# Plain norms transposed by products with a diagonal, their weight applied to feature columns: two transformer blocks on one Trainium2 core

## What is computed

```python
def _rms_norm(x, g):
    xf = x.astype(jnp.float32)
    y = xf * lax.rsqrt(jnp.mean(xf * xf, axis=-1, keepdims=True) + EPS)
    return (y * g.astype(jnp.float32)).astype(x.dtype)

for layer in range(DEPTH):
    hf = _swiglu(_rms_norm(x, g[0]), ...)
    x = x + 0.5 * _rms_norm(hf, g[1])
    xn = _rms_norm(x, g[2])
    mix = _attn_mixer(xn, ...) if layer % 2 == 0 else _mlstm_mixer(xn, ...)
    x = x + _rms_norm(mix, g[3])
    hf = _swiglu(_rms_norm(x, g[4]), ...)
    x = x + 0.5 * _rms_norm(hf, g[5])
```

## Time and profile before

| | us |
|---|---|
| median of 3 runs | 2288.61 |
| lowest, highest | 2287.96, 2290.32 |
| the profiled execution, its time | 2296.82 |
| the profiled execution, its span | 2294.6 |
| TensorE busy | 2102.6 |
| VectorE busy | 1347.0 |
| ScalarE busy | 1133.9 |

### The profile page before, as it was taken

One profiled execution on the slowest core, in us unless ns is written; L12 is line 12 of the kernel. 1 busy time (PEld: TensorE's weight loads), 2 busy tenths in 40 slices (PEclk: granted clock), 3 DMA queues, 4 the chain that ended last, 5 costly groups with the idle time before them and its releaser, 6 DMA issues.

```text
span 2294.6 us, 31170 instructions
## 1 busy us (share of the span) xinstructions
PE 2102.6 (92%) x13138; PEld 1825.3 (80%) x13138; DVE 1347.0 (59%) x1274; ACT 1133.9 (49%) x1455; POOL 446.4 (19%) x305
## 2 busy tenths in 40 slices
PE   7998977999899899699989977999998986999997
PEld 5898967999899898699978666777776875877775
DVE  5676336556665574655653656666666247565665
ACT  4765455565566354456543434454453244454553
POOL 2783000475166100036610000000000000000000
PEclk9999988999999898799999988999998787999999
DMA  9897514787688554278754105778886203688874
GB/s 325 290 310 236 168 56 135 243 280 251 210 287 277 154 167 138 94 240 293 264 175 151 56 10 211 280 287 321 340 295 222 83 1 146 235 313 316 321 290 177
DMA packets 224571, 495.98 MB, mean 216 GB/s; under 512 B 11816, under 2 KB 167576, under 8 KB 199696
## 3 DMA queue, kind: packets, MB, share of 16 engines
q1 hardware_dynamic: 200608, 410.20, 52.1%
q0 software_dynamic: 23552, 82.75, 10.6%
q10 hardware_dynamic: 272, 1.05, 0.1%
HBM read 486.57 MB, written 12.10 MB: 217 GB/s over the span
## 4 chain that ended last, share of the span: by engine, by line
PE 82%; DVE 9%; ACT 3%; DMA 3%; issue 2%; POOL 1%; DVEq 0%; SPq 0%; ACTq 0%
PE psum L972 79%; DVE nrm L2009 2%; DMA big<-in_ada_w 1%; DVE low L2009 1%; PE psum L1034 1%; DMA ring<-in_ffn_w_up 1%; PE psum L1555 1%; ACT wh L1644 1%; PE psum L1211 1%; DVE nrm L2075 0%; DVE xl L2009 0%; DVE nrm L2083 0%; DMA ring<-in_moe_w_gate 0%; DVE nrm L2073 0%; POOL big L744 0%
## 5 line engine op out<-in xcount | busy, mean ns | idle before, releaser
L2009 DVE TENSOR_TENSOR low<-ring,wh 128x2048 fp32r<-128x2048 f32 (+2 forms) x338 | 805.9, 2400 | 541.3 <-ACT wh L1644 540.2
L1644 ACT ACTIVATE wh<-ring 128x2048 fp32r<-128x2048 f32 (+2 forms) x338 | 640.6, 1903 | 430.2 <-PE psum L972 227.0
L972 PE MATMUL psum<-xh,wh 128*128 128x256 f32 x1832 | 521.6, 285 | 10.7 <-DVE low L2009 7.2
L972 PE MATMUL psum<-xl,wh 128*128 128x256 f32 x1832 | 520.8, 284 | 0.0
L972 PE MATMUL psum<-xh,low 128*128 128x256 f32 x1832 | 518.1, 283 | 0.0
L972 PEld LDWEIGHTS psum<-xh,wh 128*128 128x128 f32 x1832 | 352.8, 193 | 16.8 <-issue 9.9
L744 POOL TENSOR_TENSOR big<-big 128x1024 f32<-128x1024 f32 x144 | 306.0, 2125 | 240.9 <-ACT big L1721 232.9
L972 PEld LDWEIGHTS psum<-xl,wh 128*128 128x128 f32 x1832 | 350.9, 192 | 1.4
L972 PEld LDWEIGHTS psum<-xh,low 128*128 128x128 f32 x1832 | 351.1, 192 | 0.0
L972 PE MATMUL psum<-wh,xh 128*128 128x256 f32 (+5 forms) x864 | 278.5, 322 | 8.0 <-DVEq L647 6.0
L972 PE MATMUL psum<-wh,xl 128*128 128x256 f32 (+5 forms) x864 | 277.9, 322 | 0.0
(11 more groups left out here) (339 smaller groups left out, 2387.7 us busy)
## 6 DMA issues: line engine op xcount, KB each, us to landing
ring<-in_moe_w_gate SPq DMA_DIRECT2D x64, 1024.0 KB, 6.0
ring<-in_moe_w_up SPq DMA_DIRECT2D x64, 1024.0 KB, 6.3
ring<-in_moe_w_down SPq DMA_DIRECT2D x64, 1024.0 KB, 5.9
big<-in_ada_w POOLq DMA_DIRECT2D x48, 1024.0 KB, 6.7
ring<-in_ffn_w_gate SPq DMA_DIRECT2D x44, 1024.0 KB, 5.9
ring<-in_ffn_w_up SPq DMA_DIRECT2D x44, 1024.0 KB, 6.1
ring<-in_ffn_w_down SPq DMA_DIRECT2D x44, 1024.0 KB, 5.2
ring<-in_mlstm_w_in SPq DMA_DIRECT2D x16, 1024.0 KB, 5.5
```

The source lines that it names most:

```text
L972: return pe.matmul(out_, lhsT, rhs, start=start, stop=stop, **kw)
L1644: act.activation(wh[n % PARTS][:, 0:w], ring[SLOT_OF[n]][:, 0:w], ACT.Copy).then_inc(high, 1)
L2009: return dve.tensor_tensor(out_, a, b, op)
```

## The change

For the six plain norms (`by_columns`), `nrm` is no longer written. DVE makes, per tile, a 128x128 diagonal with the reciprocal roots on it. In the turn TensorE multiplies `x` itself by that diagonal (a real fp32 product in place of a transpose), so PSUM holds the transposed tokens already divided by their root. The norm's weight is loaded as one number per feature, [128, 8], and applied when the bank is emptied: ACT and DVE each make four instructions of 128x128 per quarter, with the weight of that feature group as a scale per partition, where each made one of 128x512. `gain_used` of the norm is raised after the turn instead of before it. The diff also carries a branch for norms with a shift (`column_vector`, `shifted`, `shifted_part`, three pieces of code); `by_columns` is false for all of them, so it does not run and is left out here.

```diff
+        def by_columns(s):
+            return STAGES[s][0] == "norm" and STAGES[s + 2][0] != "router" and not STAGES[s][1][0]
+        def diagonal(s, t):
+            g = sum(u for _, _, u in STAGES[:s])
+            return gain[g % GAINBUFS][:, P * (t + 1):P * (t + 2)]
@@ POOL, load_gain
-                pool.dma_start(gain[k % GAINBUFS][:, :], src).then_inc(gain_in[k % GAINBUFS], 16)
+                if k in COLUMNS:
+                    pool.dma_start(gain[k % GAINBUFS][:, 0:KT], GAINS[k].rearrange("(k p) -> p k", p=P),
+                                   allow_slow_non_contiguous=True)\
+                        .then_inc(gain_in[k % GAINBUFS], 16)
+                else:
+                    pool.dma_start(gain[k % GAINBUFS][:, :], src).then_inc(gain_in[k % GAINBUFS], 16)
@@ TensorE, turn
-                        last = pe.transpose(psum[:, q, i * P:(i + 1) * P], nrm[:, t, f:f + P], ident)
+                        if s and by_columns(s - 1):
+                            last = mm(psum[:, q, i * P:(i + 1) * P], x[:, t, f:f + P],
+                                      diagonal(s - 1, t), True, True)
+                        else:
+                            last = pe.transpose(psum[:, q, i * P:(i + 1) * P], nrm[:, t, f:f + P], ident)
@@ ACT, turn_columns
+                for q in range(4):
+                    tokens = slice((q // 2) * P, (q // 2 + 1) * P)
+                        act.wait_ge(turned, 4 * k + q + 1)
+                        for i in range(4):
+                            f = 4 * (q % 2) + i
+                            ins = act.activation(xh[:, f, tokens], psum[:, q, i * P:(i + 1) * P], ACT.Copy,
+                                                 scale=cols_[:, f:f + 1])
+                    ins.then_inc(turn_high, 1)
@@ DVE, norm_columns
+                for t in range(TT):
+                    dve.wait_ge(squared, SQ0[s] + t + 1)
+                    link(dve.reciprocal(stat[:, t:t + 1], stat[:, t:t + 1]))
+                    mark(dve.tensor_scalar(diagonal(s, t), ident, stat[:, t:t + 1], None, ALU.mult),
+                         normed, 2 * ran(s, "norm", "final") + t + 1)
@@ DVE, turn_columns
+                    for q in range(4):
+                        tokens = slice((q // 2) * P, (q // 2 + 1) * P)
+                        dve.wait_ge(turn_high, 4 * k + q + 1)
+                        for i in range(4):
+                            f = 4 * (q % 2) + i
+                            ins = dve.scalar_tensor_tensor(out=xl[:, f, tokens], in0=psum[:, q, i * P:(i + 1) * P],
+                                                           scalar=cols_[:, f:f + 1],
+                                                           in1=xh[:, f, tokens].bitcast(F32),
+                                                           op0=ALU.mult, op1=ALU.subtract)
+                        ins.then_inc(turn_low, 1)
+                dve.wait_ge(turn_low, 4 * k + 4)
+                for _ in range(STAGES[s - 1][2]):
+                    dve.nop().then_inc(gain_used, 1)
```

More of the change, by code:

```diff
@@ L623, in build, with shifted_part, shifts_before @@
         assert len(GAINS) == sum(s[2] for s in STAGES)
+        def by_columns(s):
[3 more added lines that the diff above has]
+            return gain[g % GAINBUFS][:, P * (t + 1):P * (t + 2)]
+        def shifted_part(q):
+            return nrm[:, q // 2, 512 * (q % 2):512 * (q % 2) + 512].rearrange("p (a b) -> p a b", a=4)
+        def shifts_before(s):
+            return sum(by_columns(j - 1) and STAGES[j - 1][1][0] is not None for j in range(1, s))
+        COLUMNS = {sum(u for _, _, u in STAGES[:s]) for s in range(len(STAGES)) if by_columns(s)}
         ada_w = [big[:, SLOT * i:SLOT * (i + 1)].rearrange("p (k n) -> p k n", k=KT) for i in range(2)]
@@ L1297, in spread_vector, with column_vector @@
                 return last
+            def column_vector(g, at):
+                wait_gain(pe, g)
+                for f in range(KT):
+                    last = mm(psum[:, 4, at + f:at + f + 1], gain[g % GAINBUFS][:, f * P:(f + 1) * P],
+                              const[:, C_ONES:C_ONES + 1], True, True)
+                return last
             def norm(s, k, m):
@@ L1302, in norm @@
                         pe.wait_ge(gate_copied, k_gate(s))
[L1303 to L1304 removed]
+                    if by_columns(s):
+                        column_vector(GAIN0[s] + 1, 0)
+                        column_vector(GAIN0[s] + 2, KT).then_inc(spread_pe, 1)
+                    else:
+                        spread_vector(GAIN0[s] + 1, 4)
+                        spread_vector(GAIN0[s] + 2, 6).then_inc(spread_pe, 1)
                 elif k == 1:
@@ L1669, in norm, with turn_columns @@
                     root_mean(stat[:, t:t + 1], D).then_inc(squared, 1)
+            def turn_columns(s, k):
+                g = GAIN0[s - 1]
+                cols_ = gain[g % GAINBUFS]
+                wait_gain(act, g)
+                for q in range(4):
+                    tokens = slice((q // 2) * P, (q // 2 + 1) * P)
+                    if STAGES[s - 1][1][0] is None:
+                        act.wait_ge(turned, 4 * k + q + 1)
[3 more added lines that the diff above has]
+                                                 scale=cols_[:, f:f + 1])
+                    else:
+                        act.wait_ge(shifted, 4 * shifts_before(s) + q + 1)
+                        ins = act.activation(xh[:, 4 * (q % 2):4 * (q % 2) + 4, tokens], shifted_part(q), ACT.Copy)
+                    ins.then_inc(turn_high, 1)
             def turn(s, k):
+                if by_columns(s - 1):
+                    return turn_columns(s, k)
                 for q in range(4):
@@ L2058, in place_pads, with norm_columns @@
                     dve.tensor_scalar(m, m, -1.0, None, ALU.mult)
+            def norm_columns(s, k, m):
+                g = GAIN0[s]
+                cols_ = gain[g % GAINBUFS]
+                wait_gain(dve, g)
+                if m is not None:
+                    dve.wait_ge(spread_pe, SPREAD0[s] + 1)
+                    dve.scalar_tensor_tensor(out=cols_[:, KT:2 * KT], in0=psum[:, 4, 0:KT], scalar=1.0,
+                                             in1=cols_[:, 0:KT], op0=ALU.add, op1=ALU.mult)
+                    link(dve.tensor_copy(cols_[:, 2 * KT:3 * KT], psum[:, 4, KT:2 * KT]))
+                for t in range(TT):
[3 more added lines that the diff above has]
+                         normed, 2 * ran(s, "norm", "final") + t + 1)
+                if k == 1:
+                    place_pads()
@@ new lines, in turn_columns, with low_of @@
+            def turn_columns(s, k):
+                g = GAIN0[s - 1]
+                cols_ = gain[g % GAINBUFS]
+                if STAGES[s - 1][1][0] is None:
+                    for q in range(4):
[8 more added lines that the diff above has]
+                        ins.then_inc(turn_low, 1)
+                else:
+                    def low_of(q):
+                        f, tokens = 4 * (q % 2), slice((q // 2) * P, (q // 2 + 1) * P)
+                        dve.wait_ge(turn_high, 4 * k + q + 1)
+                        tt(xl[:, f:f + 4, tokens], shifted_part(q), xh[:, f:f + 4, tokens].bitcast(F32),
+                           ALU.subtract).then_inc(turn_low, 1)
+                    for q in range(4):
+                        dve.wait_ge(turned, 4 * k + q + 1)
+                        for i in range(4):
+                            f = 4 * (q % 2) + i
+                            ins = dve.tensor_scalar(shifted_part(q)[:, i], psum[:, q, i * P:(i + 1) * P],
+                                                    cols_[:, KT + f:KT + f + 1],
+                                                    cols_[:, 2 * KT + f:2 * KT + f + 1], ALU.mult, ALU.add)
+                        ins.then_inc(shifted, 1)
+                        if q:
+                            low_of(q - 1)
+                    low_of(3)
+                dve.wait_ge(turn_low, 4 * k + 4)
+                for _ in range(STAGES[s - 1][2]):
+                    dve.nop().then_inc(gain_used, 1)
```

5 lines of the change are left out of this document (added).

## The result

| | before | after |
|---|---|---|
| median, us (same chip) | 2291.51 | 2302.2 |
| lowest, highest | 2287.96, 2298.0 | 2299.8, 2306.61 |
| ratio, 95% interval | 1 | 1.0044 (1.0028 to 1.006) |
| profiled execution, its span | 2294.6 | 2302.7 |
| TensorE busy, us | 2102.6 | 2113.6 |

The change makes the kernel slower by 0.44%, about 10 us (6 to 14). A second measurement of the same changed kernel gave 1.0052 (1.0039 to 1.0065). The forecast of 2288.4 meant no change, and its range of 2281 to 2296 doesn't hold the measured 2302.2.

A forecast was written before the change was run, and what follows sets the result against it. TensorE, busy 2102.6 of 2294.6 us, was taken as the bound, with pauses and half clock at seams. Start +1.3, five seams +7.5 and clock -9.0 gave -0.2 us: 2288.4 from the median of 2288.6, range 2281 to 2296.

The forecast's parts named there:

- Part 1: Each seam: TensorE starts the turn 1.67 us earlier, a reciprocal and a 0.24 us diagonal replacing VectorE's passes.
- Part 2: Turn at each seam: fp32 products take twice the transposes' time; third quarter ready after 24 passes, 5.38 us, 0.46 later.
- Part 3: Copies in four pieces at each seam: ACT's quarter 1.17 us (+0.56), VectorE's 1.12 (+0.42).
- Part 4: Clock at the seams: unbroken turn work brings full clock back before the weight products; -9.0 us together (-6 to -11).
- Part 5: Program start: the first turn ends later, delaying the first weight pieces and what follows; +1.3 us (0 to 3.4).
- (a): Rival, seams: the clock never falls, passes take 0.11 us; all five seams -10.5 us, 2278; chance 0.14.
- (b): Rival, seams: the clock doesn't come back during the turn, so its gain is gone; 2297.4 us; chance 0.10.
- (c): Rival, start: the first norm weight, loaded in 4-byte pieces, lands 6.8 us late; 2295 us; chance 0.06.
- (d): Rival, seams: copy pieces don't overlap, 4 us more, 2292.4, or 2295 with a poor mLSTM seam; chance beyond 2293 0.04.
- "Slower": Outcome for the whole kernel: measurably slower, where measurement tells apart about 0.2%, 4.6 us; chance 0.20.

The follow-up runs named there:

- e7: Kernel before, with fp32 products of `nrm` with the identity instead of transposes at the five seams; ratio 1.0006 (0.9992 to 1.002).
- e3: Kernel before, with four idle 128x512 VectorE additions ahead of the first turn's last subtraction; ratio 1.001 (0.9996 to 1.0024).
- e2: Changed kernel with only the first norm changed, the five seam norms as before; ratio 1.0019 (1.0003 to 1.0035).
- e4: Kernel before, with VectorE's two norm passes fused into one at the five seams and the last norm; ratio 0.998 (0.9968 to 0.9991).
- e9: Kernel before, with two idle 128x512 VectorE additions ahead of the first turn's last subtraction; ratio 1.0022 (1.0007 to 1.0038).
- e10: Kernel before, with four idle VectorE additions in the first turn and bias-row spreads held until the first gate piece is used; ratio 1.0014 (1.0003 to 1.0024).
- e11: Kernel before, with VectorE's two norm passes fused and bias-row spreads held until the first gate piece is used; ratio 0.9981 (0.9968 to 0.9994).
- e8: Kernel before, with ACT's and VectorE's copies in four pieces, scaled by ones, at the five seams; ratio 1.0038 (1.0021 to 1.0055).
- e1: Changed kernel with the first norm left as before, the five seam norms changed; ratio 1.0018 (1.0004 to 1.0032).
- e5: Changed kernel, with bias-row spreads held until the first gate piece is used; ratio 1.0044 (1.0029 to 1.006).
- e12: Changed kernel as it is, measured a second time against the kernel before; ratio 1.0052 (1.0039 to 1.0065).
- e13: Changed kernel, with bias-row spreads held until the first gate piece is used, measured a second time; ratio 1.0039 (1.0026 to 1.0052).

## Why the prediction was wrong

**Part 1 was right.** The turn starts 1.60 us earlier (3.34 to 1.74), forecast 1.67. The diagonal took 0.30 against 0.24.

**Part 2 was right.** 24 passes took 5.30 us, forecast 5.38. By itself the product costs 1.2 to 1.5 us in four seams and 2.3 in the first (e7).

**Part 3 was right.** ACT's quarter took 1.15 (1.17 forecast), VectorE's 1.14 (1.12). The sum of parts 1 to 3 was +7.5, and the five pauses grew by 6.3.

**Part 4 was the term that failed most: it was counted as -9.0 us, and the clock gave back nothing on balance.** That the new turn brings the clock up was right: behind all seams the clock is up when the products start. But what that gives is the difference to what a turn of transposes usually has, and that I had read from a single profile, of an execution 8.2 us slower than the median to which I carried the sum. At 377 I took 185.48 - 183.00. The same run in a kernel with the turn of transposes, the next one, and the mLSTM's, from the chain of e3:

```profile
399.13 183.15 PE psum L972 x1308
595.84 184.45 PE psum L972 x1308
793.85 21.62 PE psum L972 x144
```

At 377 the 183.15 came again within 0.02 in e2, e4, e9, e10 and e11, and 184.75 in e8: the profile of before is the slowest of all there, and the usual gain is 0 and not 2.48. At 577 it is 184.6 - 183.1 = 1.5 instead of 2.04 (184.6 is the mean of e2, e3, e9 and e10). At 215 the projection is a run of 576 products. It took 70.22 in e2; in the chains of before and of after it reads:

```profile
228.59 69.78 PE psum L972 x576
```

```profile
237.88 68.25 PE psum L997 x576
```

That is 1.5 to 2.0, as forecast, of which 1.2 are left when the attention's last run of products starts (127.8 us from the one start to the other, 129.0 in e2, e3, e9 and e10, means). At 781, where I took 3.0, there was none: 23.24 against 23.29, and against the 21.62 of e3 a loss of 1.6. The reason is in the stretches above: the clock came up some 3 us ahead of the products and fell 0.5 us into them, where the forecast had let it last 3.3.

One place isn't in the forecast at all. From the start of the mLSTM's 480 products to that of the next 168 it was 98.9 to 99.6 us in e2, e3, e9 and e10, and 101.7 to 101.9 in all five profiles whose seams are those of the change, with the same code. The clock falls earlier there. The same 5 us, 62 us behind the start of the 480, in before, e2 and after:

```profile
899.05:904.05 5.00, 3.72 (x15) 2.80 (x16) 4.77 (x9) 1.44 (x7) 0.58 (x1) 0.69 0.07 27
```

```profile
903.15:908.15 5.00, 3.17 (x18) 2.46 (x18) 4.77 (x9) 1.44 (x7) 0.58 (x1) 1.00 0.07 25
```

```profile
907.32:912.32 5.00, 3.24 (x15) 2.47 (x16) 4.77 (x9) 1.44 (x7) 0.58 (x1) 0.74 0.06 12
```

Before's own profile is among the slow ones (101.52), so the forecast couldn't see it; what decides it is open (e7, e8 and e4 are slow there too, e11 is not). That is 2.7 us more. The clock's terms are then -1.2, 0, -1.5, +1.6 and +2.7: a loss of 1.6 us where the forecast had a gain of 9.0. The whole stretch with the five seams, from the end of the first feed-forward to the products at 1174 us before, shows the same:

| profiles | us |
|---|---|
| seams as in before, delayed start: e2, e3, e9, e10 | 952.4 to 954.1 |
| before | 959.3 |
| seams of the change: after, e1, e5, e12, e13 | 960.9 to 962.7 |
| e7 (products), e8 (pieces) | 958.3, 965.8 |
| e4, e11 (one pass) | 952.0, 950.8 |

Against the first row the changed seams cost 8.3 us (pauses 6.6 in the mean of the five, clock 1.6), against before's own profile 1.6 to 3.4. e1's time gave +4.1 (0.9 to 7.3), between the two. Before has one profile only, so whether its usual executions are like the first row isn't shown; that the profiled one was 8.2 us slower than the median speaks for it. The stretch behind 1174 us, which no run changed but for the last norm, took 1112 to 1124 us in these profiles, so totals of single profiles can't settle it.

The Trainium skill's rule ("TensorE: Matmul & The Clock Gate", Part 4: PE-mode transpose), that transposes don't engage the full clock, remains against the traces. Seams of e3 that have transposes alone in the turn reach it, as this stretch right behind one shows:

```profile
399.10:401.00 1.90, 1.87 (x16) 1.90 (x17) 0.90 (x2) 1.90 (x2) 0.94 (x2) 1.00 0.75 248
```

But fp32 products bring it more surely here: the run at 577 took 183.05 to 183.23 in every kernel with the new turn, and 184.45 to 185.35 behind transposes in all but e4.

**Part 5 failed as well, in a path that it left out.** +1.3 us (at most 3.4) became 4.4 by e2's time (0.7 to 8.0), 1.35 or 8.7 in the two profiles of the same kernel. I had followed the lateness through ACT's and VectorE's splits, and let everything later move with it. The step "VectorE, the bias rows and the adaLN loads of the chain follow from there" missed that two independent queues issue side by side here: GpSimd's spreads didn't move (34.36 before, 34.12 after), SyncE's gate piece did (31.33 to 35.38), and they changed places. That this is what makes a delay of 3 us into 8 is likely and not shown, as said above. "Later work in this stage is limited by DMA, and two 512 KB loads less may hide some" didn't come either: e3, which keeps those loads, ended its feed-forward no later than after (222.89 and 223.52), and just ahead of the late request the DMA engines sat nearly idle. In the DMA share of after:

```profile
DMA  2000000000110100100004565655679999999999
```

(29 to 42 us in 40 slices, in tenths.) Every buffer of the ring held a piece that was not used up yet, so nothing was asked for.

**The rivals.** (a) didn't come: the 24 passes took 5.30 us, 0.22 each, so they ran at half clock. (b) didn't come at the feed-forwards. (c) didn't come: VectorE's first reciprocal, at 12.78, waited for ACT's root, and the loads of 4-byte pieces landed in time, in the DMA view of 0 to 14 us:

```profile
gain<-in_norm_g POOLq DMA_DIRECT2D x2, 4.0 KB, 7.6
```

The Trainium skill ("DMA: Bandwidth & Descriptors", Rules for kernel authors) advises against such loads; at this size and with 4 us to spare they cost nothing here, and in the other seams no wait for them shows. (d) didn't come as written: the pieces overlap; its side remark of a poor mLSTM seam did. "Slower" had its chance from (b), (c) and (d), and what came was none of them: a start that was late by more than itself, and a clock whose usual state before was better than in the one profile.

## What to carry to other kernels

A term that is a difference between two states of the clock must not be taken from one profiled execution: compare the same run of products over several seams, or several kernels, and take the usual one. Where a step at the start moves, look for each DMA queue that is fed by another engine and ask which of its transfers the moved step will now meet: here delays up to about 3 us cost themselves, and at a little more, with the issue 1.2 to 1.3 us behind a burst of 1.5 MB, they cost 8. Two passes of VectorE on the path are first to be fused into one, which gives no other engine more to do, before work is moved to TensorE and into smaller copies.

## What was not expected of the hardware

- The same kernel, the same seam: the granted clock came up at 30.3 us in one execution and at 32.4 in another, and runs of 1308 equal products behind the same turn took 183.15 in one and 185.48 in another. This alone is about as large as the effects at issue.
- A 1 MB load issued 1.3 us behind 1.5 MB of spreads landed after 14.9 us; half a microsecond behind them after 12.0, issued ahead of them after 5.3 to 5.9.
- A product of 128 columns with an identity in place of a transpose costs twice the passes, and still the kernel was within 0.06% of before (-0.08% to 0.2%); in its profile the runs of products behind four of the five seams took less than in before's.
- The same code of the mLSTM took 98.9 or 101.7 us, by where the granted clock fell, more than 100 us behind the last seam.
